# Head norms: the sums of squares as two rounded products over a pair made by ScalarE and GpSimd, in place of one fp32 product

## The reference

```
def rms_norm_2(x, g):
    xf = x.astype(jnp.float32)
    y = xf * lax.rsqrt(jnp.mean(xf * xf, axis=-1, keepdims=True) + NORM_EPS)
    return (y * g.astype(jnp.float32)).astype(x.dtype)

q = apply_rope(rms_norm_2(q.reshape(B, S, DA_HEADS, 2, HEAD_DIM), q_norm), cos, sin)
k = apply_rope(rms_norm_2(k.reshape(B, S, DA_HEADS, 2, HEAD_DIM), k_norm), cos, sin)
```

## Time and profile before

| | us |
|---|---|
| median of 3 runs | 1882.84 (1881.79 to 1883.13) |
| span of the profiled execution | 1880.6 |
| PE busy | 1863.9 (99%) |
| DVE busy | 1124.2 (60%) |
| ACT busy | 778.9 (41%) |
| POOL busy | 278.1 (15%) |

### The profile page before, as it was taken

One profiled execution on the slowest core, in us unless ns is written; L12 is line 12 of the kernel. 1 busy time (PEld: TensorE's weight loads), 2 busy tenths in 40 slices (PEclk: granted clock), 3 DMA queues, 4 the chain that ended last, 5 costly groups with the idle time before them and its releaser, 6 DMA issues.

```text
span 1880.6 us, 24035 instructions
## 1 busy us (share of the span) xinstructions
PE 1863.9 (99%) x9258; PEld 1490.0 (79%) x9258; DVE 1124.2 (60%) x1782; ACT 778.9 (41%) x1728; POOL 278.1 (15%) x217
## 2 busy tenths in 40 slices
PE   9999999999999999999999999999999999999999
PEld 6887777888888888777688888888866788888887
DVE  7555885754454465588875445445978765445343
ACT  6435776332232232476643223223357533223221
POOL 2000551211010121111021101101210111011010
PEclk9999999999999999999999999999999999999999
DMA  6231000333333233322133332332332123333333
GB/s 230 59 104 63 24 2 20 93 101 96 95 101 93 98 90 101 102 78 77 48 102 92 99 101 92 99 101 82 104 107 63 62 90 101 95 96 101 92 94 95
DMA packets 51536, 166.52 MB, mean 89 GB/s; under 512 B 6880, under 2 KB 7264, under 8 KB 51168
## 3 DMA queue, kind: packets, MB, share of 16 engines
q1 hardware_dynamic: 51424, 165.00, 28.7%
HBM read 155.01 MB, written 2.10 MB: 84 GB/s over the span
## 4 chain that ended last, share of the span: by engine, by line
PE 91%; DVE 6%; ACT 1%; issue 1%; DMA 1%; SPq 1%; POOL 0%; DVEq 0%; ACTq 0%
PE bank L987 25%; PE bank L989 25%; PE bank L988 24%; PE bank L1097 2%; PE bank L1157 2%; PE bank L961 2%; PE bank L962 2%; PE bank L963 2%; DVE WL L1622 1%; PE bank L1010 1%; PE bank L1187 1%; PE bank L1199 1%; PE bank L1235 1%; PE bank L1212 1%; PE bank L1125 1%
## 5 line engine op out<-in xcount | busy, mean ns | idle before, releaser
L1302 ACT ACTIVATE WH<-RAW 128x512 fp32r<-128x512 f32 (+2 forms) x584 | 331.8, 613 | 772.0 <-PE bank L989 687.8
L1622 DVE TENSOR_TENSOR WL<-RAW,WH 128x512 fp32r<-128x512 f32 (+2 forms) x584 | 458.9, 822 | 75.7 <-ACT WH L1302 69.7
L987 PE MATMUL bank<-GH,WH 128*128 128x512 f32 x1088 | 433.1, 398 | 0.6 <-DVE GL L1908 0.6
L987 PE MATMUL bank<-HH,WH 128*128 128x512 f32 x1056 | 422.0, 400 | 2.4 <-DVE HL L1637 1.3
L989 PE MATMUL bank<-GH,WL 128*128 128x512 f32 x1088 | 423.9, 390 | 0.0
L988 PE MATMUL bank<-GL,WH 128*128 128x512 f32 x1088 | 423.6, 389 | 0.0
L989 PE MATMUL bank<-HH,WL 128*128 128x512 f32 x1056 | 411.6, 390 | 0.0
L988 PE MATMUL bank<-HL,WH 128*128 128x512 f32 x1056 | 411.3, 389 | 0.0
L2169 POOL TENSOR_TENSOR TMP<-TMP,RST 128x512 f32<-128x512 f32 x66 | 116.2, 1761 | 864.9 <-DVE TMP L2079 864.9
L987 PEld LDWEIGHTS bank<-GH,WH 128*128 128x128 f32 x1088 | 204.4, 188 | 45.2 <-issue 3.5
L988 PEld LDWEIGHTS bank<-GL,WH 128*128 128x128 f32 x1088 | 204.5, 188 | 43.1 <-issue 2.6
(11 more groups left out here) (252 smaller groups left out, 1889.7 us busy)
## 6 DMA issues: line engine op xcount, KB each, us to landing
RAW<-in_wgu SPq DMA_DIRECT2D x132, 512.0 KB, 3.5
RAW<-in_wd SPq DMA_DIRECT2D x48, 512.0 KB, 3.5
RAW<-in_wd SPq DMA_DIRECT2D x24, 384.0 KB, 3.1
RAW<-in_da_qk SPq DMA_DIRECT2D x16, 512.0 KB, 3.6
TMP<-TMP SPq DMA_DIRECT2D x104, 64.0 KB, 2.0
RAW<-in_w_inh SPq DMA_DIRECT2D x12, 512.0 KB, 3.7
RAW<-in_w_out SPq DMA_DIRECT2D x8, 512.0 KB, 3.7
RAW<-in_da_v SPq DMA_DIRECT2D x8, 512.0 KB, 3.5
```

The source lines that it names most:

```text
L987: e.matmul(b, w_h, hi[st.x][k], start=(k == 0), stop=False)
L1302: e.activation(whs[s % NW][:, a:b], raw[s % NR][:, a:b], ACT.Copy).then_inc(S["wh"], 1)
L1622: e.tensor_tensor(wls[s % NR][:, a:b], raw[s % NR][:, a:b], whs[s % NW][:, a:b].bitcast(F), ALU.subtract).then_inc(S["wl"], 1)
```

## The change

ACT squares each unit twice: once into SQB in fp32, once into a new buffer SR in fp32r. POOL subtracts the second from the first (`qsl`), which gives the rest of the square, in fp32r too. PE then makes two fp32r products with a matrix of ones in fp32r (BR), added up in bank 3, in place of the one fp32 product. POOL makes BR once, at the start. The plan's costs for these steps are new, and one need is added to the plan: in the stages with stationary tokens a unit's first four triples come after those of the unit before. `qsq` of the first norm of `ks` also waits for work that frees the place of SR.

```
@@ -338,8 +338,9 @@
-        o.add("ACT", ("qsq", *at), 500, of(st, m))
-        o.add("PE", ("qst", *at), 960, ("qsq", *at), st == "in" and ("lz4", 0), take=("nb", ("nr", *at)))
+        o.add("ACT", ("qsq", *at), 1000, of(st, m))
+        o.add("POOL", ("qsl", *at), 1300, ("qsq", *at))
+        o.add("PE", ("qst", *at), 520, ("qsl", *at), st == "in" and ("lz4", 0), take=("nb", ("nr", *at)))
@@ in dense(), stages with stationary tokens @@
-                          operand(name, k), k == 0 and bank_before(name, i), u > 0 and t == 4 * st.per - 1 and last[u - 1],
+                          operand(name, k), k == 0 and bank_before(name, i), ul and t < 4 and ("tri", name, u - 1, t), u > 0 and t == 4 * st.per - 1 and last[u - 1],
@@ -1005,9 +1013,11 @@
             def qst(st, m):
                 g = NM[st] + m
-                p.wait_ge(S["nm_sq"], g + 1)
+                p.wait_ge(S["nm_lo"], g + 1)
+                p.wait_ge(S["br"], 1)
                 norm_bank("nm_nr", g + 1)
-                e.matmul(nb, bones, sqb[1], start=True, stop=True).then_inc(S["nm_st"], 1)
+                e.matmul(nb, BR[:, :], sq_hi[st], start=True, stop=False)
+                e.matmul(nb, BR[:, :], sq_lo[st], start=False, stop=True).then_inc(S["nm_st"], 1)
@@ -1347,8 +1357,12 @@
+                if st == "ks" and m == 0:
+                    p.wait_ge(S["vl"], SP_["s"])
+                    p.wait_ge(S["op"], OP["h4"] + 8)
                 b = ST[st].banks[m % len(ST[st].banks)]
                 e.activation(sqb[1], bank[b], ACT.Square).then_inc(S["nm_sq"], 1)
+                e.activation(sq_hi[st], bank[b], ACT.Square).then_inc(S["nm_sq"], 1)
@@ -2115,11 +2129,18 @@
+                p.wait_ge(S["cf"], 16)
+                e.tensor_copy(BR[:, :], bones).then_inc(S["br"], 1)
...
+            def qsl(st, m):
+                p.wait_ge(S["nm_sq"], 2 * (NM[st] + m + 1))
+                p.wait_ge(S["nm_st"], NM[st] + m)
+                e.tensor_tensor(sq_lo[st], sqb[1], sq_hi[st].bitcast(F), ALU.subtract).then_inc(S["nm_lo"], 1)
```

More of the change, by code:

```diff
@@ L651 @@
     "in_o vg_o hv_o h3_o h3_t h3_v wo_o dv_o qk_o do_o ks_o vs_o sq_o so_o "
-    "nm_sq nm_st nm_nr nm_rs nm_cs nm_q sw0 sw1 ks0 ks1 rope_v rope_a kt gain ci zeros zp "
+    "nm_sq nm_lo nm_st nm_nr nm_rs nm_cs nm_q sw0 sw1 ks0 ks1 rope_v rope_a kt gain ci zeros zp "
     "gt_v gt_a gt lam_v lam_a lam lb_v lb_a lb ns "
@@ L656 @@
     "hg_k hg_ln hg_lk hg_b hg_bk hg_sv hg_sp hg_ex hg_mp hg_mm hg_bm hg_at hg_kd hg_ke hg_qe hg_eb hg_eq hg_ks "
-    "hg_wi hg_wc hg_ov hg_mix xh warm first0 first1 raw0 raw1 raw2 raw3 raw4 gp x0 x1 x2 x3 x4 x5 x6 x7 cf cb pos cii w1k w1v w2 outs"
+    "hg_wi hg_wc hg_ov hg_mix xh br warm first0 first1 raw0 raw1 raw2 raw3 raw4 gp x0 x1 x2 x3 x4 x5 x6 x7 cf cb pos cii w1k w1v w2 outs"
 ).split()
@@ L688, in program @@
         first_only.close()
+        pairs_only = ExitStack()
+        pairs_only.enter_context(nc.sbuf_tensor("PAD", [128, 12 * T], F))
+        SR = pairs_only.enter_context(nc.sbuf_tensor("SR", [128, 8 * T], R))
+        pairs_only.close()
         PX = sbt("PX", 22 * T)
@@ L692, in program @@
         CF = sbt("CF", C_N)
+        BR = sbt("BR", 128, R)
         CB = sbt("CB", 128 * 5, BF)
@@ L721, in program @@
         squares = tmp + pb[4:6]
+        sq_hi, sq_lo = [{st: SR[:, (c + k) * T:(c + k + 1) * T] for st, c in (("in", 0), ("qk", 6), ("ks", 2), ("sq", 2))}
+                        for k in range(2)]
         def p1(a, n):
@@ L2169, in ff_scale @@
                 e.tensor_tensor(s, s, RST[:, :], ALU.mult).then_inc(S["ff_y"], 1)
-            steps = {"pag": accumulate, "zerosg": consts, "cs": cs, "zero": zero, "decg": dec, "dech": dec_queries,
+            steps = {"pag": accumulate, "zerosg": consts, "cs": cs, "qsl": qsl, "zero": zero, "decg": dec, "dech": dec_queries,
                      "eqmg": wh0, "nad": nad, "e_gug": ff_scale}
```

## The result

The changed kernel takes 1887.51 us (median of 7 runs, 1885.79 to 1891.23) beside 1882.63 us (7 runs, 1881.79 to 1883.14) for the kernel before. The ratio is 1.0027, with a 95% interval of 1.0018 to 1.0036: slower by 4.9 us, where 9.4 us faster was forecast. The time lies outside the range. Of all runs in this document two, one of the kernel before (10651.53 us) and one with the subtraction on DVE (2304.17 us), were disturbed and are left out.

What follows compares the result with a forecast made beforehand. PE's queue was taken as the bound, busy for 1863.9 of 1880.6 us. The terms -13.7 + 3.3 + 0.5 + 0.5 = -9.4 us took 1882.8 to 1873.4 us, with a range of 1868.5 to 1878.5 at 0.83.

Steps and rivals of the forecast that it cites:

- PE is the bound: Whole kernel: PE is busy for 1863.9 of 1880.6 us and holds 91% of the chain that ended last.
- What is removed and added on PE, -13.7: All 32 norms: fp32 products at 0.88 us go (28.2 us), pairs of fp32r products at 0.227 us each come (14.5 us).
- Casting BR at nothing: POOL, behind the first `qsl`: over 5 us are left for a subtraction and a small cast, so it costs nothing.
- Second square hidden: ACT, all norms: 32 x 0.5 = 16 us on an engine busy for 41% of the span, costing nothing as busy time.
- the rival of many waits: Later norms of `qk` and `sq`: PE waits 0.5 to 1 us at ten of 22 norms; 1877 to 1882 us, chance 0.18.
- Three waits of 1.0 to 1.2 us on `qn`, and none at the other norms: First two norms of `qk`, first of `sq`: PE waits 1.1 us each for the bank, 3.3 in all; the others pay nothing.
- The second norm of `in`, 0.2 to 0.7: Second pair of products in `in`: PE waits 0.6 to 1.1 us; net cost 0.2 to 0.7, taken as 0.5.
- With 6.8 us less PE work beside them, I add 0.5 us there and in `sq` together, between 0 and 4: Late `qk` and `sq`: PE loses filler beside attention's own chains; 0.5 us added, between 0 and 4.
- DVE's contention at 0.04: Rival "Slower", `qk`, `ks`, `sq`: 26 POOL subtractions lengthen DVE's split, 28 us, DVE becomes the bound; 1901 us, chance 0.04.
- my three signs of being wrong: PE waits at `qk` pairs beyond the third norm; DVE's split grows over a few per cent; first-attention wait changes over 1 us.
- POOL's subtractions are hidden as busy time: POOL, all norms: 32 subtractions of 1.3 to 1.8 us, 42 to 57 us, on an engine with 85% of the span free.
- The rival of dear rounded products: The pairs: two rounded products cost 0.86 us each, as much as the fp32 one; 1882.8 + 27 us, chance 0.01.

Runs made afterwards that it cites:

- the one with costs 900 and 1200: Changed kernel with only the planner's costs lowered, squares 1000 to 900 ns and subtraction 1300 to 1200 ns, and the order with them: 1880.99 us, ratio 0.9990.

## Why the prediction was wrong, point by point

- **PE is the bound.** Right before, and half right after: its queue still sets the end, but with 86% of the chain in place of 91%.
- **What is removed and added on PE, -13.7.** The fp32 product was priced well (28.0 us read in the new order, 28.2 forecast). The pair was under-sized by 1.5 us: 0.454 was taken for all 32 and holds for 18; at thirteen of the 17 that stand next to attention's small matmuls it is 0.54 to 0.64. What came through was 10.4. The L1010 group is replaced as foreseen, though records near 390 and 430 ns say nothing of the price, since they overlap:

```profile
L1019 PE MATMUL bank<-SR,BR 128*128 128x512 f32 x32 | 13.7, 429 | 1.4 <-POOL SR L2143 1.4
L1020 PE MATMUL bank<-SR,BR 128*128 128x512 f32 x32 | 12.5, 392 | 0.0
```

- **Casting BR at nothing.** Right. It ends at 31.2 on POOL, and the product that needs it starts at 34.83:

```profile
30.49 0.75 POOL L2133 CAST BR<-CF 128x128 fp32r<-128x128 f32 x1
```

- **Second square hidden.** Right: +0.6 us. It did stand ahead of exponentials at 911, as the rival of many waits had it, but with little effect by itself.
- **Three waits of 1.0 to 1.2 us on `qn`, and none at the other norms.** Right in place and size for the three. But `qn` has three more waits, 0.17 us at 788.63, 0.58 at 878.45 and 0.88 at 1393.73, 1.6 us that were put at nothing. The first of the three forecast, in PE's order of time:

```profile
770.85 0.39 PE L1019 MATMUL bank<-SR,BR 128*128 128x512 f32 x1
771.07 0.39 PE L1020 MATMUL bank<-SR,BR 128*128 128x512 f32 x1
...
773.11 0.39 PE L997 MATMUL bank<-GH,WL 128*128 128x512 f32 x1
774.45 0.47 PE L995 MATMUL bank<-GH,WH 128*128 128x512 f32 x1 [0.95 <-DVE TMP L1745]
```

  From 773.11 to 774.45 are 1.34 us, less 0.23 is 1.11; the second of `qk` and the first of `sq` have 1.11 and 1.12 in the same way. The pair starts 3.40 us behind the time called 0 there (767.45), as forecast. `qsl` there took 1.30 and no more, and 1.74 for the second to fourth norm:

```profile
768.81 1.30 POOL L2143 TENSOR_TENSOR SR<-SQB,SR 128x512 fp32r<-128x512 f32 x1 [48.87 <-ACT SR L1365]
...
775.63 1.74 POOL L2143 TENSOR_TENSOR SR<-SQB,SR 128x512 fp32r<-128x512 f32 x1
```

- **The second norm of `in`, 0.2 to 0.7.** Right, at its upper end. The matmul ahead of the pair starts 1.31 us before it, 1.08 more than back to back, where it was 0.38 before: 0.7 net.

```profile
37.11 0.39 PE L997 MATMUL bank<-HH,WL 128*128 128x512 f32 x1
38.42 0.50 PE L1019 MATMUL bank<-SR,BR 128*128 128x512 f32 x1 [0.92 <-POOL SR L2143]
```

- **"With 6.8 us less PE work beside them, I add 0.5 us there and in `sq` together, between 0 and 4": the step that failed.** It priced the attention stages by the waits that the old order had. But the whole order of `qk` and `sq` was laid out anew around a longer chain, and that alone costs 7.0 us with the old work. Only 3.9 of it are at `qn`, and 2.7 of those at the forecast's three norms. That less work on PE also leaves more of a softmax's chain bare is likely but not shown by itself: in the same order 1.6 of 12.0 us did not come through. From the first matmul of `qk`'s first triple to the last matmul of the projection behind its attention the trace has 212.0 us before and 214.3 after, with 6.8 us less work on PE; from `sq` to `so` 153.0 and 155.8, with 3.4 less.
- **DVE's contention at 0.04: the second step that failed.** The rival's price was right in kind. I read the pair of halves at 2.38 us in place of 1.29, multiplied by 26, and asked whether DVE would become the bound as a whole. It did not. DVE lost 16.8 us, not 28, and the time rose by 5.8. None of my three signs of being wrong came: PE does not wait for POOL at any pair of `qk`, and the first attention's waits are unchanged (1.3 us behind ACT's copies of its weights in both). The one on the split (more than a few per cent) was badly chosen, for its mean grew from 835 to 853 ns, 2.2%, and the loss was there. The argument against it, that PE works three to four units behind the weights, covers the split alone. It does not cover the steps of a softmax, for which PE waits at once. That POOL's subtractions are hidden as busy time was therefore right for POOL and wrong for the kernel.
- **The wait at the pair itself.** Forecast once, at the second norm of `in`, with 0.5 us net. It comes there and again at the fourth norm of `in` (0.50 us at 52.35), which was not foreseen. The runs put +1.7 us on it, a difference within scatter.
- **Slips in the working.** `qk` and `sq` have 24 of the 32 norms; 26 counts `ks` too. Idle time on PE was to rise by 4 us and rose by 14.6, or 13.3 without the missing records. The rival of dear rounded products would have made the kernel slower, so its 0.01 belongs to the chance of slower. None of this moves the sum.

The sum: losses of 7.0 + 0.6 + 5.8 + 1.7 = 15.1 us, where 4.3 were forecast, and a gain of 10.4 in place of 13.7. The 10.8 and the 3.3 are the 14.1 us between 1873.4 and 1887.5, to the rounding. Two losses are shown by runs that change nothing else: that of the order, whose inner working stays open, and that of the contention, whose places in the trace are given above. The rivals *Many new waits* and *Slower* were both at work, each for a part; I had treated them as exclusive. Not settled is which waits beyond `qn` make up the order's 7.0 us, and why neighbouring costs move the time by 3 to 6 us.

## What to carry to other kernels

When a planner makes the order, price the new order apart from the new work: build the old work in the new order first. Three versions here that differ only in two cost numbers lie up to 6.5 us apart, more than the change itself moved the time. And work moved to GpSimd is not free because GpSimd is idle: count every VectorE instruction with two SBUF operands that it will overlap, and ask which of those an engine waits for at once, not how busy VectorE is on average.

Of the versions with the full work, the one with costs 900 and 1200 and the one with the subtraction on DVE are the best, 0.1% under the kernel before.

## What the hardware showed that I had not expected

- A POOL subtraction of 128x512 that overlaps a DVE instruction of 128x256 made that one 0.96 us long in place of 0.48, a full doubling, while it took only 1.28 us itself. Another one made an addition of 128x512 1.79 us long in place of 0.68. With the weights' split it is POOL that stretches too, 1.74.
- 32 subtractions on DVE add 19.8 us to its busy time; the same 32 on POOL add 16.0 us to DVE's busy time. Handing the work over saved DVE a fifth of it (the two orders differ).
- A rounded product of 128x512 takes 0.227 us between others of its shape and 0.31 to 0.34 us behind small matmuls or a wait.
